# Weight remainders of a two-layer block plus an RWKV layer: made by adding DMAs instead of by GpSimd

## The reference, cut to what matters

```python
for i in range(2):
    h = _rmsnorm(hres, norm_g[i, 0])
    m = _diff_attention(h, ...) if i % 2 == 0 else _short_conv(h, ...)
    hres = hres + _rmsnorm(m, norm_g[i, 1])
    h = _rmsnorm(hres, norm_g[i, 2])
    hres = hres + _rmsnorm(_sqrelu_mlp(h, w_up[i], w_down[i]), norm_g[i, 3])
x = hres[:, 16:]
z = rmsnorm(x) @ w_in          # third block: 25 column blocks of 128
x = rmsnorm(x + y @ w_out)     # y: pooled and time-mixed features
```

## Time and profile before

| | us |
|---|---|
| median of 3 runs (lowest to highest) | 1612.18 (1611.86 to 1613.28) |
| profiled execution, its span | 1610.8 |
| what lies around the span, by the median | 1.4 |
| TensorE busy | 1556.7 |
| VectorE busy | 784.8 |
| ScalarE busy | 620.5 |
| GpSimd busy | 527.8 |

### The profile page before, as it was taken

How to read it: one execution, slowest core, us unless ns; L and a number is a source line. 1 busy time by engine, 2 the same in 40 slices (tenths; PEclk the granted TensorE clock), 3 DMA queues, 4 the chain that set the end, 5 groups by cost and what they waited for, 6 DMA issues and landing times.

```text
span 1610.8 us, 31514 instructions
## 1 busy us (share of the span) xinstructions
PE 1556.7 (97%) x12758; PEld 1389.2 (86%) x12758; DVE 784.8 (49%) x1372; ACT 620.5 (39%) x1142; POOL 527.8 (33%) x235
## 2 busy tenths in 40 slices
PE   8999998999999999999999999999999989999997
PEld 7898988999999999999989888888889867787766
DVE  5444444754132231575446642322316899656655
ACT  5666665443232231442224532322224534433322
POOL 2222222044444444124440444444441234450011
PEclk9999999999999999999999999999999989999999
DMA  5111121222222222223222222232222222200001
GB/s 200 49 58 53 54 66 54 66 94 92 93 94 93 93 95 90 74 80 105 91 91 80 86 98 92 93 102 94 92 92 80 66 86 85 91 17 3 3 27 52
DMA packets 35691, 125.69 MB, mean 78 GB/s; under 512 B 4080, under 2 KB 4336, under 8 KB 35568
## 3 DMA queue, kind: packets, MB, share of 16 engines
q1 hardware_dynamic: 35568, 123.90, 23.6%
HBM read 121.79 MB, written 2.10 MB: 77 GB/s over the span
## 4 chain that ended last, share of the span: by engine, by line
PE 69%; DVE 9%; issue 4%; ACT 2%; POOL 1%; DMA 0%; POOLq 0%; DVEq 0%; SPq 0%; ACTq 0%
PE G L1509 58%; PE G L1844 2%; PE ST L1844 2%; PE PO L1844 1%; PE PV L1844 1%; DVE wlo L946 1%; DVE t L1248 1%; POOL wlo L474 1%; DVE m L966 1%; PE ST L1475 1%; PE ST L1509 1%; DVE hres L973 1%; DVE z L1251 1%; DVE z L1233 0%; DMA raw<-weights_dram 0%
## 5 line engine op out<-in xcount | busy, mean ns | idle before, releaser
L474 POOL TENSOR_TENSOR wlo<-raw,whi 128x1024 fp32r<-128x1024 f32 x207 | 502.0, 2426 | 1050.1 <-ACT whi L530 735.2
L1509 PE MATMUL G<-xh,whi 128*128 128x258 f32 (+3 forms) x1504 | 366.9, 306 | 9.3 <-DVE wlo L946 4.1
L1509 PE MATMUL G<-xl,whi 128*128 128x258 f32 (+3 forms) x1504 | 357.4, 300 | 0.0
L1509 PE MATMUL G<-xh,wlo 128*128 128x258 f32 (+3 forms) x1504 | 355.9, 299 | 1.1 <-DVE xl L914 1.1
L1509 PE MATMUL G<-ah,whi 128*128 128x256 f32 (+2 forms) x1024 | 278.3, 313 | 1.9 <-DVE al L1133 1.6
L1509 PE MATMUL G<-ah,wlo 128*128 128x256 f32 (+2 forms) x1024 | 276.5, 311 | 0.0
L1509 PE MATMUL G<-al,whi 128*128 128x256 f32 (+2 forms) x1024 | 276.4, 311 | 0.0
L1509 PEld LDWEIGHTS G<-xh,whi 128*128 128x128 f32 x1504 | 242.5, 189 | 32.7 <-issue 10.5
L1509 PEld LDWEIGHTS G<-xh,wlo 128*128 128x128 f32 x1504 | 243.8, 188 | 10.9 <-DVE xl L914 1.3
L540 ACT ACTIVATE whi<-raw 128x1024 fp32r<-128x1024 f32 x96 | 101.8, 1061 | 388.3 <-PE G L1509 388.3
L1509 PEld LDWEIGHTS G<-xl,whi 128*128 128x128 f32 x1504 | 242.9, 188 | 9.8
(11 more groups left out here) (347 smaller groups left out, 2000.6 us busy)
## 6 DMA issues: line engine op xcount, KB each, us to landing
raw<-weights_dram SPq DMA_DIRECT2D x225, 512.0 KB, 3.7
hres<-xT_dram SPq DMA_DIRECT2D x8, 264.0 KB, 5.2
out_dram<-hres SPq DMA_DIRECT2D x8, 256.0 KB, 2.3
con<-consts_dram SPq DMA_DIRECT2D x1, 512.0 KB, 7.4
mat<-mats_dram SPq DMA_DIRECT2D x1, 512.0 KB, 8.1
con<-consts_dram SPq DMA_DIRECT2D x1, 264.0 KB, 6.6
vec<-vecs_dram SPq DMA_DIRECT2D x1, 171.0 KB, 6.3
con<-consts_dram SPq DMA_DIRECT2D x1, 128.0 KB, 4.2
```

What stands on the lines that cost most here:

```text
L474: nc.gpsimd.tensor_tensor(wlo[:, s], raw[:, s % 2], whi[:, s].bitcast(F32), ALU.subtract)\
L1509: last_of[0] = nc.tensor.matmul(to[:, p0:p1], wt[:, w, ws], xt[:, k, t0 - off:t1_ - off], start=k == 0 and q == 0, stop=k == KT - 1 and q ...
```

## The change

ScalarE makes two passes over `raw`: the rounded block into `whi`, and the negative of the rounded block into `wlo` (an activation with scale -1.0, whose result is rounded on the way out). Then a DMA that GpSimd issues adds the weights from HBM onto `wlo`, which leaves weights minus rounded weights. GpSimd subtracts nothing. Blocks whose remainder VectorE makes are as before. `hi_ready` now means that both passes are done; each slot of `wlo` has a semaphore of its own, `lo_landed`, that counts 16 for each added block; SyncE waits for `hi_ready` instead of `lo_ready` before it refills `raw`, and its loop and GpSimd's are written out. To have semaphores for that, some of VectorE's single-use ones are merged; order and waits there stay.

```diff
+        def rounded_on_vector(b):
+            return b < 2 or any(0 <= b - new < HELD for new in (32, 96, 128, 192))
+        def wait_low(eng, b, s=None, segment=0):
+            if isinstance(b, int) and rounded_on_vector(b):
+                eng.wait_ge(lo_ready, sum(rounded_on_vector(i) for i in range(b + 1)))
+                return
+            s, segment = (b % 4, b) if isinstance(b, int) else (s, segment)
+            other = sum(rounded_on_vector(i) for i in range(s, segment, 4))
+            eng.wait_ge(lo_landed[s], 16 * (b // 4 + 1 - other) if isinstance(b, int) else (b - s) * 4 + 16 * (1 - other))
...
-                sp.wait_ge(lo_ready, b - 1)
+            for b in range(2, NBLK):
+                if rounded_on_vector(b - 2):
+                    wait_low(sp, b - 2)
+                else:
+                    sp.wait_ge(hi_ready, b - 1)
+                sp.dma_start(raw[:, b % 2], weights[b]).then_inc(w_loaded[b % 2], 16)
...
-                if not isinstance(b, int) or b >= 4:
-                    pool.wait_ge(block_done, b - 3)
-                nc.gpsimd.tensor_tensor(wlo[:, s], raw[:, s % 2], whi[:, s].bitcast(F32), ALU.subtract)\
-                    .then_inc(lo_ready, 1)
+                pool.dma_start(wlo[:, b % 4], weights[b], accum_op=ALU.add).then_inc(lo_landed[b % 4], 16)
...
+            def rounded(b, s):
+                hi = nc.scalar.activation(whi[:, s], raw[:, s % 2], ACT.Copy)
+                if isinstance(b, int) and rounded_on_vector(b):
+                    hi.then_inc(hi_ready, 1)
+                else:
+                    nc.scalar.activation(wlo[:, s], raw[:, s % 2], ACT.Copy, scale=-1.0).then_inc(hi_ready, 1)
...
-                pe.wait_ge(lo_ready, b + 1)
+                wait_low(pe, b, s, segment)
```

More of the change, by code:

```diff
@@ L240, in program @@
         hi_ready = sem("hi_ready"); lo_ready = sem("lo_ready")
+        lo_landed = [sem(f"lo_landed{i}") for i in range(4)]
         block_done = sem("block_done"); tile_out = sem("tile_out")
@@ L450, in _ @@
             sp.dma_start(mat[:], mats).then_inc(mat_loaded, 16)
-            def load(b, j, s):
-                if isinstance(b, int) and b < 2:
-                    return
-                sp.wait_ge(lo_ready, b - 1)
-                src = weights[b] if isinstance(b, int) else weights[bass.ds(b, 1)].rearrange("b p n -> p (b n)")
-                sp.dma_start(raw[:, s % 2], src).then_inc(w_loaded[s % 2], 16)
-            blocks(sp, 0, NBLK, load)
+            for b in range(2, NBLK):
[4 more added lines that the diff above has]
+                sp.dma_start(raw[:, b % 2], weights[b]).then_inc(w_loaded[b % 2], 16)
             for k in LAST_ORDER:
@@ L469, in _, with low @@
         def _(pool):
-            def low(b, j, s):
+            def low(b):
                 pool.wait_ge(hi_ready, b + 1)
-                if not isinstance(b, int) or b >= 4:
-                    pool.wait_ge(block_done, b - 3)
-                nc.gpsimd.tensor_tensor(wlo[:, s], raw[:, s % 2], whi[:, s].bitcast(F32), ALU.subtract)\
-                    .then_inc(lo_ready, 1)
[L477 to L484, removed]
+                pool.dma_start(wlo[:, b % 4], weights[b], accum_op=ALU.add).then_inc(lo_landed[b % 4], 16)
+            for b in range(2, B_O2 + 3):
+                if not rounded_on_vector(b):
+                    low(b)
             pool.wait_ge(tile_out, B_IN2 + 17)
@@ L512, in _ @@
                 n += 2
-            blocks(pool, B_O2 + 3, KT - 3, low)
+            for b in range(B_O2 + 3, B_O2 + KT):
+                low(b)
             pool.wait_ge(S("rstd_copied"), len(BESIDE) + 1)
@@ L529, in split @@
                         act.wait_ge(block_done, b - 3)
-                nc.scalar.activation(whi[:, s], raw[:, s % 2], ACT.Copy).then_inc(hi_ready, 1)
+                rounded(b, s)
+            def rounded(b, s):
[4 more added lines that the diff above has]
+                    nc.scalar.activation(wlo[:, s], raw[:, s % 2], ACT.Copy, scale=-1.0).then_inc(hi_ready, 1)
             def step(b0, n, evac=None):
@@ L1515, in keep_busy, with begin @@
                     nc.tensor.matmul(place[:, 0:P], ident, ones, start=True, stop=True)
-            def begin(b, fifth=False):
-                pe.wait_ge(lo_ready, b + 1)
+            def begin(b, s, segment, fifth=False):
+                wait_low(pe, b, s, segment)
                 if not isinstance(b, int) or b >= 2:
@@ L1606, in body @@
                 def body(b, j, s, lead=False):
-                    begin(b, start is not None and isinstance(j, int) and j == HELD)
+                    begin(b, s, b0 + 4, start is not None and isinstance(j, int) and j == HELD)
                     for k in range(KT):
@@ L1751, in _ @@
             first_sums(1)
-            pe.wait_ge(lo_ready, 2)
+            wait_low(pe, 1)
             some(G[1], 1, range(2), xh, xl, 0, part(ALL))
@@ L1850, in _ @@
                     ahead = j + 2 if j < 4 else j
-                    pe.wait_ge(lo_ready, B_IN2 + ahead + 1)
+                    wait_low(pe, B_IN2 + ahead)
                     pe.wait_ge(tile_out, B_IN2 + ahead - 3)
```

44 lines of the change are left out of this document (22 added, 22 removed).

## The result

The changed kernel takes 1664.76 us (median of 4 runs, 1661.95 to 1667.95) against 1612.73 of the kernel before on the same chip: a ratio of 1.0317, 95% interval 1.0304 to 1.0330. It is slower by 52 us; forecast were 26, range 1608 to 1688. The profiled execution spans 1662.9 us, 52.1 more than the one before.

What follows compares the result with a forecast made beforehand. It took TensorE, busy 1556.7 of 1610.8 us, to bound the kernel. From the median 1612.2, start 2, attention 11, fifth blocks 11.8 + 4.6, clock 8 and features -11 gave +26: 1638 us, range 1608 to 1688.

Steps and rivals of the forecast that it cites:

- the fifth blocks: Blocks 36, 100, 132 and 196, where TensorE already waits for the remainder: 4.6 us later each, all on the path.
- Nothing at 6.0: Last four blocks of four products: slot free 8.6 us ahead against 8.2 needed, so no cost; 5 each at 11.4.
- the landing L: Time from GpSimd's wake-up to the adding DMA's last semaphore: put at 6.0 us, between 3.4 and 11.4.
- SyncE refills raw 1.4 us sooner after whi: Long products: refill 2.2 us after whi instead of 3.6, two loads a block sharing the DMA engines; counted as nothing.
- Rival 3: Additions fill the DMA engines, so the long products run at the DMAs' pace: about 1780 us; chance 9%.
- Start, +2 forecast: Block 2: remainder 3.7 us late, of which 1.65 comes back at the first scores' result: +2.0 us.
- Attention, +11 forecast: Second ScalarE pass: 1.0 us for each of 6 heads, 0.7 at the third scores of about 7 heads.
- 2 us each: TensorE's granted clock falls after each of the four waits of about 5 us: 4 x 2 = 8 us lost.
- Features, -11 forecast: Features stage: VectorE freed of GpSimd's reads, TensorE's waits of 6.8 and 1.5 us and 3 us of low clock go.
- Rival 4: Features: descriptor writing by GpSimd still slows VectorE; gain 0 to 5 instead of 11, 1643 to 1649 us; no separate chance.
- Rival 1: Early landing: the addition is as quick as a load, 3.4 us, giving 1618 us; chance 13%.
- Rival 2: Faster: VectorE's relief wins, with landing near 3.4 us and passes hidden in attention: 1607 us; chance 16%.

Runs made afterwards that it cites:

- experiment 6: Changed kernel, but SyncE refills raw only when the addition of the block two before has landed: 1771.76 us, ratio 1.0980 to the kernel before.
- experiment 5: Changed kernel, but GpSimd's DMA only copies the weights over wlo and adds nothing: 1638.83 us, ratio 1.0159 to the kernel before.
- Experiment 2: Changed kernel, but GpSimd subtracts every block as before, and ScalarE's second pass is made and overwritten: 1630.37 us, ratio 1.0112 to the kernel before.
- experiments 4, 9 and 10: Changed kernel with additions and second passes only from block 197, from 199, and from 199 with 201 subtracted (GpSimd subtracts the rest): 1606.71, 1603.87, 1603.05 us.

## Why the prediction was right or wrong

The sign and the mechanism were right: a later remainder where TensorE already waits, a second pass on the path in attention, VectorE's relief in the features. The size was off by half: 52 us against 26. By the table, the miss is +15.5 between the fifth blocks (ends of products and the clock), +3.7 at the start, +3.8 at the fifth blocks, -2.9 in attention, +2.3 in the features and +3.3 behind them. The main step that failed is "Nothing at 6.0" for the ends of products; what pushed it over was the landing L, set at 6.0 and measured at 7.8.

**The term L was too small, and it is no constant.** The step "L = 3.7 + 1.4 + 0.9 = 6.0" took each part from a row in which the loads ran alone. Its parts alone were fair, though the 1.4 was low (171 ns is the mean over all packets of the queue, 3952 of 4 bytes among them; those of 4 KB took 201 ns, 1.6 us a block): without a load beside it the addition lands in 5.5 us (experiment 6), from 0.86 of issue, 3.09 of data in each engine (36.1% of 1772.1 over 207) and the rest latency. What was missing is the sentence that I wrote and counted at nothing: "SyncE refills raw 1.4 us sooner after whi, the two loads a block share the engines". It wakes on the same event as GpSimd, and the two lie on each other: 7.8 instead of 5.5 us for the addition. The loads go from 3.7 to 6.1, because additions that long also meet the transfers of the next block. A common start alone is not the cause; with the shorter copy of experiment 5 it costs the load nothing. At the fifth blocks L was 6.8, 7.6, 6.4 and 6.9, and they cost 22.2 us instead of 18.4. In the long products load and addition were forecast to take 4.1 of a block's 5.7 us; by the DMA share of 0.89 they take 5.1 (an estimate, 0.89 x 5.7). Rival 3 was nearer than its 9% said, though TensorE kept its 119 ns a matmul, and experiment 6 went over an edge that is the slot's and not the engines'.

**Ends of products, "Nothing at 6.0", failed.** The margin was 8.6 us against 8.2. With the measured landing it is gone; the timeline of the changed kernel at the end of the first MLP:

```profile
682.26 1.06 ACT L540 ACTIVATE whi<-raw 128x1024 fp32r<-128x1024 f32 x1 [3.22 <-PE G L1523]
...
684.56 0.86 POOL L485 DMA_DIRECT2D wlo<-weights_dram  x1 [4.89 <-ACT wlo L544]
...
693.57 0.45 PE L1523 MATMUL G<-ah,whi 128*128 128x258 f32 x1 [2.77 <-DMA wlo<-weights_dram]
```

2.3 + 9.0 = 11.3 us, 2.7 over the 8.6. The other ends wait 2.45 + 1.09, 1.82 (behind one of 0.16) and 1.33, 9.6 us in all. With the clock that falls behind the waits, what lies between the fifth blocks came to 19.5 us (6.7 + 5.0 + 6.0 + 1.8) where the sum had 4. This is the largest error, 15 of the 26 us, and experiment 5 shows the cause: with a landing of 4.8 us the waits at the ends are gone. A margin of 0.4 us under an unknown of 3.4 to 11.4 should have been priced by its chance, not at nothing.

**Start, +2 forecast, +5.7 measured.** The step assumed that 1.65 us come back at the first scores, and L = 6.0. TensorE waits 6.67 us for block 2:

```profile
23.06 1.00 POOL L485 DMA_DIRECT2D wlo<-weights_dram  x1 [22.63 <-ACT wlo L544]
...
31.18 0.81 PE L1523 MATMUL G<-xh,whi 128*128 128x272 f32 x2 [6.67 <-DMA wlo<-weights_dram]
```

L is 8.1 here, with the input loads still coming (the DMA share of 12 to 32 us is 0.70). The 1.65 us do come back, but 1.6 are lost behind the wait, where the granted clock is 0.50 from 31 to 34 us; the step left that out.

**Attention, +11 forecast, +8.1 measured.** Against the earlier trace rows:

```profile
110.52 1.04 ACT L540 ACTIVATE whi<-raw 128x1024 fp32r<-128x1024 f32 x1
111.47 1.04 ACT L544 ACTIVATE wlo<-raw 128x1024 fp32r<-128x1024 f32 x1
112.41 0.67 ACT L736 ACTIVATE ah<-ST,gsub 128x514 fp32r<-128x514 f32 x1
...
113.11 0.75 DVE L1147 SCALAR_TENSOR_TENSOR al<-ST,gsub,ah 128x514 fp32r<-128x514 f32 x1 [2.06 <-ACT ah L736]
...
114.02 0.46 PE L1668 MATMUL G<-kT,qT 64*128 64x264 f32 x1 [1.00 <-DVE al L1147]
```

1.0 us six times, as forecast; at the third scores 0.3 us instead of 0.7, seven times. Experiment 2 shows the same six waits with no adding DMA in the kernel, so they are the pass alone.

**Clock.** "2 us each" behind the fifth blocks held roughly: from 360 to 364 us TensorE starts 25 matmuls where 33 go at full clock (4 us by 119 ns), 1.0 us lost, and the us between 359.10 and 360 was slower still. Both profiles have the same 12758 matmuls in the same order, so each can be set beside its partner: the first of block 36 comes 25.98 us later than before (359.10 against 333.12), the one 24 places on 27.57 (363.65 against 336.07). That is 1.6 us for the clock; behind blocks 100, 132 and 196 it is 2.0, 1.6 and 2.0, together 7.2 where the sum had 8. Another 1.6 us each are lost behind the waits of 2.45, 2.77 and 1.82 us at the ends, for which the sum had nothing.

**Features, -11 forecast, -6.7 measured** (-9 with the clock). VectorE's relief is whole, against the earlier trace rows:

```profile
1320.36 0.75 DVE L1265 SCALAR_TENSOR_TENSOR z<-t,vec,z 128x512 f32<-128x512 f32 x1
...
1321.75 0.75 DVE L1265 SCALAR_TENSOR_TENSOR z<-t,vec,z 128x512 f32<-128x512 f32 x1
```

and so is it in the MLPs (the subtraction for `al`, line 1041 before, 1055 after, fell from 1.86 to 0.69 us), where it is worth nothing, as said. But new waits of 0.25, 1.63 and 0.69 us stand in the stage. Rival 4 falls: GpSimd's issues do not hold VectorE up. Rival 1 falls with the landing. Rival 2 was right about VectorE's relief and not about the kernel as a whole: alone, in experiments 4, 9 and 10, the relief makes a faster kernel.

**Behind the features, 0 forecast, +3.3 measured.** The output's last matmul comes 1.4 us later than the end of the features would have it, and GpSimd's DRAIN adds the 1.8 shown above. That instruction took 2.6 us in the kernel before and in experiment 2, where GpSimd issues no DMA, 4.7 to 4.9 with 25 to 28 additions, 5.9 with 181, 7.8 to 8.1 with 203 to 207, and 10.5 with the 207 copies, where it ends 4.4 us after SyncE's. What it does in that time no run shows.

The Trainium skill (Collectives: The Full Stack, The bandwidth ceiling) says of the reduction step of a collective that it runs at half the rate of a copy because it reads two sources. The additions here agree: 2.95 us of each engine against 1.46 of the copy.

The Trainium skill's sum for a plain transfer issued by GpSimd (DMA: Bandwidth & Descriptors, Anatomy of one DMA — SWDGE (gpsimd) path) gives 3.2 us for these bytes. Here the measurement differs: the quickest copy of experiment 5 took 3.8 us and the median 4.8.

What stays open: how the landing of 9.0 us at the end of a product divides between engine time and its queue, why an addition suffers more from a load beside it than a copy does, and what GpSimd's DRAIN waits for.

## What to carry to other kernels

When work moves from an engine to DMAs, look at which event releases the new DMA, what else that event releases, and whether the transfers of one round are over when the next begins: here additions of 5.5 us took 7.8 once loads ran beside them, and additions of 7.8 met those of the next block. And a buffer or a margin of 0.4 us that is "just enough" under an unknown duration should be priced as a wait with its chance. Two small delays that share a margin cost more together than their sum. Freeing an engine pays only in the stretch where it, or an engine that it slows, ends last; make the change there alone.

## What the runs showed of the hardware

- An adding DMA of 512 KB from HBM onto SBUF: 0.86 us of GpSimd's time, 2.95 to 3.09 us of each of 16 engines, 5.5 us to landing without loads beside it, 7.8 with. The plain copy: 0.53, 1.46, and 4.8 us to landing with a load beside it.
- A load of 512 KB that starts 0.3 us ahead of the copy lands in 3.8 us, against 3.7 with no copy; with an addition in the copy's place the loads' median is 6.1.
- GpSimd's closing DRAIN takes 2.6 us where it issued no DMA, 8.0 behind 207 additions and 10.5 behind 207 copies.
- VectorE's subtraction for `al` (128 x 512 to 514) took 1.86 us on average with GpSimd subtracting beside it and 0.69 with GpSimd only issuing DMAs.
- TensorE's granted clock is 0.67 over the four us behind a wait of 5.84 us, and full in the next four.
